# Two modulation columns moved from the attention to the up stage, and idle products among the transposes

## The reference, cut to what matters

```python
mod = c @ w_ada[l] + b_ada[l]
sh1, sc1, gt1, sh2, sc2, gt2 = jnp.split(mod, 6, axis=-1)
h = rms_norm(x, g_pre_mix[l]) * (1.0 + sc1[:, None]) + sh1[:, None]
proj = h @ w_in[l]
...
o = jnp.concatenate([o_nsa, o_dsa], axis=-1) @ w_out[l]
x = x + gt1[:, None] * rms_norm(o, g_post_mix[l])
h = rms_norm(x, g_pre_ffn[l]) * (1.0 + sc2[:, None]) + sh2[:, None]
y = jnp.square(jax.nn.relu(h @ w_up[l])) @ w_down[l]
x = x + gt2[:, None] * rms_norm(y, g_post_ffn[l])
```

## Time and profile before

| | us |
|---|---|
| median of 3 runs | 1531.42 |
| lowest and highest | 1527.2, 1542.44 |
| the profiled execution's own time | 1541.84 |
| its span in the trace | 1540.0 |

### The profile page before, as it was taken

The page is one execution under the profiler, slowest core; times in us unless marked ns, Lnnn a source line. Parts: engine busy times, 40 slices in busy tenths (PEclk is TensorE's granted clock), DMA queues, the critical chain, the costliest instruction groups (busy, mean ns, idle before and its releaser), DMA issues.

```text
span 1540.0 us, 23035 instructions
## 1 busy us (share of the span) xinstructions
PE 1444.8 (94%) x9084; PEld 1235.6 (80%) x9084; DVE 854.6 (55%) x1485; ACT 743.5 (48%) x1369; POOL 978.7 (64%) x710
## 2 busy tenths in 40 slices
PE   5798998899999899879999999999998999999998
PEld 2676656699887898559999999999997888888886
DVE  4655664445313786352589948999895333322222
ACT  2442122555545667344444455445554555555554
POOL 0564461467766453145689998877886777777775
PEclk9896896999999999989999999999999999999999
DMA  9342441444554432033544544555555666555552
GB/s 388 134 164 110 164 165 55 164 163 166 192 187 168 164 123 99 26 110 137 192 165 164 192 166 170 186 191 175 181 200 207 240 244 239 212 191 192 192 191 82
DMA packets 48588, 263.78 MB, mean 171 GB/s; under 512 B 5472, under 2 KB 14048, under 8 KB 19040
## 3 DMA queue, kind: packets, MB, share of 16 engines
q1 hardware_dynamic: 38272, 251.68, 45.3%
q10 hardware_dynamic: 10208, 10.63, 2.0%
HBM read 252.84 MB, written 9.44 MB: 170 GB/s over the span
## 4 chain that ended last, share of the span: by engine, by line
PE 62%; DVE 19%; POOL 3%; issue 1%; ACT 1%; DVEq 0%; ACTq 0%
PE bank L1385 23%; PE bank L782 21%; PE bank L748 15%; DVE arena L2608 4%; DVE hotg L2608 4%; DVE arena L2604 3%; DVE hots L2604 3%; POOL v_lo L1914 3%; PE bank L1165 1%; DVE arena L2620 1%; DVE arena L2490 1%; PE bank L763 0%; DVE hT_lo L1971 0%; PE bank L912 0%; PE bank L1331 0%
## 5 line engine op out<-in xcount | busy, mean ns | idle before, releaser
L1914 POOL TENSOR_TENSOR v_lo<-ring,v_hi 128x512 fp32r<-128x512 f32 x448 | 620.3, 1402 | 169.4 <-ACT v_hi L1814 160.4
L1906 POOL TENSOR_TENSOR v_lo<-ring,d_hi 128x512 fp32r<-128x512 f32 x213 | 291.3, 1378 | 318.4 <-ACT d_hi L1507 257.0
L1814 ACT CAST v_hi<-ring 128x512 fp32r<-128x512 f32 x512 | 315.3, 621 | 307.6 <-PE bank L1385 163.3
L748 PE MATMUL bank<-hT_hi,v_hi 128*128 128x256 f32 x1024 | 295.2, 288 | 5.3 <-POOL v_lo L1914 5.2
L748 PE MATMUL bank<-hT_lo,v_hi 128*128 128x256 f32 x1024 | 286.7, 280 | 0.0
L748 PE MATMUL bank<-hT_hi,v_lo 128*128 128x256 f32 x1024 | 286.3, 280 | 0.0
L1507 ACT CAST d_hi<-ring 128x512 fp32r<-128x512 f32 x236 | 144.3, 621 | 171.7 <-PE bank L782 150.0
L1385 PE MATMUL bank<-v_hi,mix_hi 128*128 128x512 f32 x512 | 201.9, 394 | 3.2 <-DVE mix_lo L2635 3.2
L1385 PE MATMUL bank<-v_hi,mix_lo 128*128 128x512 f32 x512 | 201.7, 394 | 0.0
L1385 PE MATMUL bank<-v_lo,mix_hi 128*128 128x512 f32 x512 | 201.7, 394 | 0.0
L748 PEld LDWEIGHTS bank<-hT_hi,v_hi 128*128 128x128 f32 x1024 | 193.0, 188 | 6.9 <-POOL v_lo L1914 6.0
(11 more groups left out here) (327 smaller groups left out, 2434.9 us busy)
## 6 DMA issues: line engine op xcount, KB each, us to landing
ring<-w_dram SPq DMA_DIRECT2D x230, 1024.0 KB, 4.8
gate_dram<-gput ACTq DMA_DIRECT2D x64, 128.0 KB, 3.2
gget<-gate_dram SPq DMA_DIRECT2D x32, 256.0 KB, 4.9
x<-x_dram SPq DMA_DIRECT2D x1, 1024.0 KB, 5.5
arena<-mem_dram ACTq DMA_DIRECT2D x1, 1024.0 KB, 11.1
out_dram<-x SPq DMA_DIRECT2D x1, 1024.0 KB, 4.0
arena<-const_dram ACTq DMA_DIRECT2D x1, 884.0 KB, 9.4
arena<-vec_dram ACTq DMA_DIRECT2D x1, 144.0 KB, 4.5
```

The costliest lines, as they stand in the source:

```text
L748: return nc.tensor.matmul(out_, lhsT, rhs, start=start, stop=stop)
L1814: nc.scalar.copy(v_hi[:, r, :], quarter(at, r)).then_inc(s_vhi, 1)
L1906: nc.gpsimd.tensor_tensor(v_lo[:, r, :], dense_quarter(d, r), d_hi[:, r, :], ALU.subtract).then_inc(s_dpl, 1)
L1914: nc.gpsimd.tensor_tensor(v_lo[:, r, :], quarter(at, r), v_hi[:, r, :], ALU.subtract).then_inc(s_plo, 1)
```

## The change

Four things are done, and one follows from them.

1. The row blocks of pieces 10 and 11 are taken out of the attention, with ACT's copies. Their four half tiles stand in the ring behind the tiles 1, 2, 3 and 4 of the up projection, and DVE weighs each after the units 3, 5, 7 and 9. TensorE sums them in the down stage ahead of its tile group 4, and the gain rows of the second half are made ahead of group 6, with ACT's copies there. Every turn of the attention now has six idle products. `MOD_AT` has six entries in place of eight, two of them at earlier turns.
2. One idle product of 128x256 (`FILLERS_TURN`) stands ahead of each of the 14 pairs of `pairT` and of each of the four of `kcT` and `vcT`.
3. TensorE may turn the first 128 tokens into features when DVE has finished their heads, and no longer waits for both halves.
4. One DVE operation on `gg` moves from the end of the attention to the down stage.
5. Since two results fewer take a bank ahead of the up stage and three more behind it, later results have other banks.

```diff
+ADA_WITH_UP = {1: ("ada", 10, 0), 2: ("ada", 10, 1), 3: ("ada", 11, 0), 4: ("ada", 11, 1)}
...
-    tiles += [("up", n, k) for n in range(8) for k in range(2)]
+    for n in range(8):
+        tiles += [("up", n, k) for k in range(2)]
+        if n in ADA_WITH_UP:
+            tiles += [ADA_WITH_UP[n]]
...
-            for m in range(4):
+            for m in range(2):
                 rotate(("gg", m), every)
...
+    rotate(("ada", 1), [0, 1, 2, 3])
+    for m in range(2, 4):
+        rotate(("gg", m), [0, 1, 2, 3])
     rotate(("mkv", 1), every)
...
-MOD_AT = {5: 4, 6: 5, 11: 11, 13: 6, 16: 7, 19: 10, 22: 8, 24: 9}
+MOD_AT = {5: 4, 6: 5, 13: 6, 14: 7, 20: 9, 22: 8}
...
+ADA_AFTER = {2 * n + 1: name for n, name in ADA_WITH_UP.items()}
 FILLERS = 6
-FILLERS_ROW = 2
 FILLERS_FIRST = 12
+FILLERS_TURN = 1
...
                 for tb in range(TB):
                     if norm is not None:
                         pe.wait_ge(s_xn, 2 * norm + tb + 1)
+                    if what == "oT":
+                        pe.wait_ge(s_o, tb + 1)
...
-                    for _ in range(FILLERS_ROW if i + 1 in ROW_BLOCKS else FILLERS):
+                    for _ in range(FILLERS):
...
-                    if i in ROW_BLOCKS:
-                        ada_row_blocks(*ROW_BLOCKS[i])
...
+                    for _ in range(FILLERS_TURN):
+                        mm(ps[:, s * T:(s + 1) * T], identb, ident[:, :].bitcast(BF16))
...
             for kg in range(8):
+                if kg == 4:
+                    pe.wait_ge(s_avec, len(ADA_VEC))
+                    ps = begin(("ada", 1))
+                    for n in (10, 11):
+                        for s in range(4):
+                            last = mm(ps[:, 4 * n + s:4 * n + s + 1], ada_sum(n)[:, s * P:(s + 1) * P], one)
+                    end(last, ("ada", 1))
+                if kg == 6:
+                    pe.wait_ge(s_ggf, 2)
+                    for m in range(2, 4):
+                        gain_rows(m)
...
-            link(tt(gg[:, 8:16], mod[:, 40:48], vall("g_post_ffn"), ALU.mult))
...
-            nc.vector.memset(coef[:, 0:1], 0.0).then_inc(s_o, 1)
+                nc.vector.memset(stat[:, 153 + tb:154 + tb], 0.0).then_inc(s_o, 1)
...
                 tt(up_lo[:, 2 * n:2 * n + 2, :], v, up_hi[:, 2 * n:2 * n + 2, :], ALU.subtract).then_inc(s_uplo, 1)
+                if n in ADA_AFTER:
+                    weigh(ADA_AFTER[n])
```

More of the change, by code:

```diff
@@ L105, in weight_tiles @@
     tiles += [("cmp1", n, 0) for n in range(2)]
[L106 to L107 removed]
+    tiles += [("ada", n + m, k) for n in (4, 6, 8) for k in range(2) for m in range(2)]
     tiles += [("out", n, k) for n in range(2) for k in range(2)]
     tiles += [("mem_kv", 0, k) for k in range(2)]
[L110 removed]
+    for n in range(8):
+        tiles += [("up", n, k) for k in range(2)]
+        if n in ADA_WITH_UP:
+            tiles += [ADA_WITH_UP[n]]
     tiles += [("down", kg, n) for kg in range(8) for n in range(2)]
@@ L126 @@
 DENSE_AT = {t: d for d, t in enumerate(DENSE)}
-ADA_ROWS = [("ada", n, k) for n in (2, 3, 11, 10) for k in range(2)]
+ADA_ROWS = [("ada", n, k) for n in (2, 3) for k in range(2)]
 ADA_POOL = [("ada", n, k) for n in range(5, 10, 2) for k in range(2)]
-ADA_VEC = [("ada", n, k) for n in (4, 6, 8) for k in range(2)]
+ADA_VEC = [("ada", n, k) for n in (4, 6, 8, 10, 11) for k in range(2)]
 WHOLE = [t for t in TILES if t not in DENSE_AT and t not in ADA_ROWS + ADA_POOL + ADA_VEC]
@@ L415, in build @@
         ggb = take(2, D)
-        addb = take(4, 512)
+        addb = take(2, 512)
         block1_end = where[0]
@@ L420, in build @@
         take(D_FF // P, T)
-        assert where[0] <= block1_end - 2 * D - 4 * 512
+        assert where[0] <= block1_end - 2 * D - 2 * 512
         sbqT = take(4, T, at=common)
@@ L841, in modulation @@
                 end(last, ("ada", 0))
[L843 to L857, removed]
             def modulation_columns(ps, n):
@@ L862, in modulation_columns @@
                     pe.wait_ge(s_avec, ADA_VEC.index(("ada", n, 1)) + 1)
-                elif ("ada", n, 1) in ADA_POOL:
+                else:
                     pe.wait_ge(s_apool, ADA_POOL.index(("ada", n, 1)) + 1)
-                else:
-                    pe.wait_ge(s_arc, 3 + (n == 10))
                 for s in range(4):
[L868 to L872, removed]
+                    last = mm(ps[:, 384 + s:385 + s], ada_sum(n)[:, s * P:(s + 1) * P], one)
                 return last
@@ L976, in _ @@
                 for g in range(2):
+                    for _ in range(FILLERS_TURN):
+                        mm(ps[:, g * T:(g + 1) * T], identb, ident[:, :].bitcast(BF16))
                     for tb in range(TB):
@@ L1058, in _, with gain_rows @@
             attention(UNITS1, operands1, values1, [(0, P), (P, P + T)], mask1)
-            pe.wait_ge(s_o, 1)
+            def gain_rows(m):
+                ps = begin(("gg", m))
+                for k in range(4):
+                    last = mm(ps[:, k * P:(k + 1) * P],
+                              gg[:, 4 * m + k:4 * m + k + 1].to_broadcast([P, P]), ident[:, :])
+                end(last, ("gg", m))
             rows_to_features("oT", osum)
@@ L1512, in attention @@
                 for i, unit in enumerate(units):
-                    if i in ROW_COPIED:
-                        n = ROW_COPIED[i]
-                        ps = wait_full(act, ("adarow", n))
-                        free(nc.scalar.copy(ada_sum(n)[0:1, :], ps[0:1, :]), ("adarow", n))
-                        wait_read(act, ("adarow", n))
-                        nc.scalar.copy(stat[:, 152:153], one).then_inc(s_arc, 1)
                     ps = wait_full(act, ("S", *unit))
@@ L1609, in _, with gain_rows @@
             high_parts(("out", 1, 1))
-            for n in range(4):
+            def gain_rows(n):
                 ps = wait_full(act, ("gg", n))
                 free(nc.scalar.copy(ggb[:, n // 2, (n % 2) * 512:(n % 2 + 1) * 512], ps[:, :]), ("gg", n))
+            for n in range(2):
+                gain_rows(n)
             row_squares("out", 2)
@@ L1625, in _ @@
                 nc.scalar.activation(up_hi[:, 2 * n:2 * n + 2, :], v, ACT.Square).then_inc(s_uphi, 1)
+            high_parts(("down", 6, 0))
+            for n in range(2, 4):
+                gain_rows(n)
             high_parts(("down", 7, 1))
```

15 lines of the change are left out of this document (7 added, 8 removed).

## The result

The changed kernel took 1558.5 us (median; five runs between 1553.4 and 1562.5, a sixth was disturbed and is left out), the kernel before, run beside it, 1532.8 us. The ratio is 1.0148, 95% interval 1.0093 to 1.0202: slower by 1.5%. The prediction was 1545, range 1527 to 1562. The sign and the range held; against that median the size was half of the truth. The profiled execution took 1558.66 us, with a span of 1556.5. It is 16.5 us longer than the span of before and not 25.6, since the profiled execution of before was itself 9 us over the median of the six runs of before that are known now.

A forecast was written before the change was run, and what follows sets the result against it. TensorE was taken as the bound (busy 94% of the span): its work, its clock and its waits for DVE or transfers. 1541.8 - 14.8 - 2.0 + 1.8 + 1.0 + 15.0 + 2.4 = 1545.2, predicted 1545 us, range 1527 to 1562.

The forecast's parts named there:

- Attention: Attention turns: less TensorE work saves 9.4 us, less time at the low clock (29 us low) saves 5.4; -14.8 us.
- Behind the attention: After the attention: removed gg operation 1.19 us, split wait for the weighted sums 0.8 us less; -2.0 us.
- Idle products among the transposes: Transposes ahead of the attention: 16 of 18 idle products on the path at 0.11 us each; +1.8 us.
- Down stage: Down stage: eight column products come, +1.0 us; gain rows move here from the output projection at no net cost.
- Up stage: Up projection: DVE releases ring slots late, so TensorE waits at tiles 3, 4 and 5; +15.0 us, bounds 10 and 19.
- A slow start of a tile is covered by the next wait: Up stage: TensorE's low clock after a wait costs only behind the last wait, 1.3 us.
- For tile 6 only half 1 is concerned, which just covers it: Up stage, tile 6: only half 1 is late, 5.9 us later in TensorE's order, so no further wait.
- The bank of the second block: Second block's first projection product must wait for the last hT_lo quarter, 2.7 us later; +2.4 us, bounds 0 and 4.
- The surplus of before: Profiled execution, 10.4 us over the median: said not to matter, lying in the attention's clock, 12 us of it taken back.
- Rival A: Up stage: the ring has room after all and the 15 us of waits do not come; 1530 us, chance 0.15.
- B: Attention turns 6 to 24: row blocks had kept the clock up; without them 1573 us; chance 0.17 of 10 us or more.
- C: Attention: the clock stays up for nearly the whole stage, 13 us less, 1532 us; chance 0.15.

The follow-up runs named there:

- e1: The changed kernel with each of DVE's four sums in the up stage placed one up tile earlier; 1545.6 us, ratio 1.0085.
- e2: The changed kernel with the second and third of four blocks left out of each sum in the up stage; 1545.1 us, ratio 1.0079.
- e3: The changed kernel with the second memory rows put back in bank 3; 1554.7 us, ratio 1.0139.
- e5: As e1, with DVE's quarter of the next half tile's low part taken between the second and third block of each sum; 1533.7 us, ratio 0.9978.
- e7: As e5 with e3's bank and e4's setting, and the transposes of the attention's output in banks 0 to 3, not 2 to 5; 1526.4 us, ratio 0.9949.
- e4: The changed kernel without the 18 idle products among the transposes ahead of the attention; 1556.9 us, ratio 1.0142.

## Why the prediction was right or wrong, by its steps

- **Attention, -14.8 forecast.** From Oc to DVE's last copy 115.9 became 102.8 us: -13.1. The sum was near, its parts were not. The clock gave nothing in this execution: mean 0.81 over 115.8 us before (44 us low) and 0.79 over 102.8 after (43 us low), where I took 29. The work gave nearly the whole 13.1; the 3.7 us that I kept back for DVE were too much, TensorE's waits in those turns being 0.68 and 1.28 us. The clock is also what scatters: with the same code up to there, e1, e2, e3 and e5 took 97.3, 99.8, 103.1 and 103.0 us, at mean clocks of 0.86, 0.82, 0.79 and 0.79.
- **Behind the attention, -2.0 forecast.** From the last copy to the first product 10.2 became 9.1: -1.2, the removed operation. The 0.8 us of the split wait did not come: I costed the wait and not the bank of the fourth oT. e7 showed it.
- **Idle products among the transposes, +1.8 forecast, +2.5 measured.** 18 x 0.11 is 2.0, and 0.5 more is lost around them. Shown by e4, with 0.7 us of it given back in the stretch behind: 1.8 in all.
- **Down stage, +1.0 forecast.** +3.6 there and -3.0 ahead of up. The gain rows moved 1.9 us from one to the other, as said. The columns take 1.8 and not 1.05: two sets of four columns, where the row is one set, counted x8 in the profile. And 0.9 us came back that I had not seen: 5.3 us from the transposes of h2T to the first product of up before, 4.4 after. The shift of the banks took h2T out of the bank of up's second unit; that this is the cause is argued from the order of the banks, and no run put it back. The two new groups in the down stage, the gain rows and the columns:

```profile
L750 PE MATMUL bank<-ident,arena 128*128 128x128 f32 x16 | 1.9, 275 | 0.0
L750 PE MATMUL bank<-stat,arena 128*128 128x1 f32 x16 | 1.8, 245 | 0.0
```

- **Up stage, +15.0 forecast, +25.2 measured. This is the term that failed by size.** The loop is the one that was forecast, and its waits ahead of tiles 3, 4 and 5 were 4.5, 4.5 and 4.3 us for forecasts of 4.5, 4.6 and 4.6. That agreement is partly luck. What the loop sets is the distance between the starts of two tiles, and I had 16.3 us (landing at 345.1, the next at 361.4) where 18.5 and 18.1 came. The step that failed first is DVE's queue ahead of the sum. From the landing to the sum I counted the four casts, relu and square, and DVE's last operations, 7.5 us; it was 9.6 us (328.25 to 337.83), since DVE had a low part (1.53) and four operations of two units (5.8) to do one after the other, three of them at 1.7 us beside POOL. The sum (4.1 us) and the transfer (4.8) were as forecast. The waits came out right all the same because TensorE, at a mean clock of 0.87 and 0.86 in tiles 3 and 4, was slower by about as much. "A slow start of a tile is covered by the next wait" held there: the loop set the pace.
- **The same term behind the last wait for a slot.** From the start of tile 5 to the down stage it was 43.8 us, against 35.7 before: 8.1 us where I had 1.3. 4.0 us are the wait ahead of the last quarter of tile 5. I had followed the sums only to the slots that they release, and never asked what stands behind a sum in DVE's queue: the low part that TensorE needs next. The fourth sum took 5.8 us where I had 4.0. "For tile 6 only half 1 is concerned, which just covers it" was right, since no wait of half a microsecond stands in tile 6. The other 4 us are the clock, 0.88 on average over these tiles: here no wait covers it. In the whole stage TensorE's idle time rose by 18.0 us, from 2.3 to 20.3, and its busy time, for the same products, by 7.1, from 93.7 to 100.8, at a mean clock of 0.92 in place of 0.98. Up to the start of tile 3, in tile 3, in tile 4 and from tile 5 on, the surplus over before is 3.97 + 6.74 + 6.34 + 8.12 = 25.17 us. e1, e2 and e5 show that it is DVE's queue, first through the slot and then through the low part.
- **The bank of the second block, +2.4 forecast, +5.0 measured.** The first product came 2.8 us later, as worked out. Then the clock was low there (0.51 over the first 6 us, 1.00 in e3): 8.8 us from it to the next product shown, against 7.0 in e3. I had priced the wait and not the clock behind it. Shown by e3.
- **The surplus of before, and luck.** I held that the profiled execution's 10 us over the median did not matter for the sum. It did. Against the profiled execution the sum says +3.4 us (1541.8 to 1545.2), and +16.8 came. The sum stood 13.8 us over the median then known, and 10.4 of these were the surplus and 3.4 the terms. That the time went the way that was forecast, and that 1558.5 lies inside the range, owes more to the surplus than to the terms. The changed kernel's own profile was at its median (1558.7 and 1558.5). If the surplus of before lay in its attention, 115.9 us in that one profile, a usual execution has some 107 there, and the change's gain in the attention is nearer to 4 us than to 13. That is argued: there is no second profile of the kernel before.

Put right, the terms give 1541.8 - 13.1 - 1.2 + 2.5 + 0.6 + 25.2 + 5.0 = 1560.8, and the 1.2, 0.4 and 0.9 us that the other stretches gave bring it to 1558.3 against 1558.66. Rival A is out (the ring had no room), and B and C did not come in this profile.

## What to carry to other kernels

When an engine that is behind in its own work is made to release a buffer, follow the loop through it: transfer, cast, its queue, the release. If it closes and is longer than the compute of a tile, every tile pays the difference, and moving the work one tile earlier in the queue can open it. In the loop, count all that the engine has queued ahead of the moved work. Then read what stands behind the moved work on that engine, and put the piece that others wait for in the middle of it. A change of the number of groups in a rotation of banks shifts every later group: print the banks of before and after and look at each place where a group is freed late. And where a loop sets the pace, a slow clock costs nothing; behind its last turn it costs in full, so price it there.

## What the hardware showed that I had not expected

DVE's time for one operation goes with whether POOL is at work. POOL's three low parts in the changed kernel's third round end at 334.07 + 4.92 = 339.0. The multiply-add on 128x512 that started at 337.83, beside them, took 1.72 us, the three that started after took 0.76 each (the chain above), and the subtraction L2295 took 0.69 and 1.67 within one round. The mean of 0.96 us from the earlier trace rows was a mixture of the two and hid a factor of 2.3. Its POOL row:

```profile
334.07 4.92 POOL L1905 TENSOR_TENSOR v_lo<-ring,d_hi 128x512 fp32r<-128x512 f32 x3 [0.91 <-ACT d_hi L1505]
```

That POOL is the cause is read from the overlap; no run took POOL's work away.
